# A fused decoder step: twelve gate-projection tiles placed between the attention units, keys without zero padding, sample values turned

## Time and profile before

| what | us |
|---|---|
| executions (median) | 713.58, 714.10, 723.62 (714.10) |
| profiled execution, its span | 716.92, 715.1 |
| TensorE busy | 667.6 (93%) |
| VectorE, ACT, POOL busy | 372.2, 271.4, 150.2 |
| TensorE on the chain that ended last | 51% of the span |
| stages: projection, attention, gates, tail | 255.6, 187.5, 256.0, 16.0 |

### The profile page before, as it was taken

How to read it: one execution, slowest core, us unless ns; L and a number is a source line. 1 busy time by engine, 2 the same in 40 slices (tenths; PEclk the granted TensorE clock), 3 DMA queues, 4 the chain that set the end, 5 groups by cost and what they waited for, 6 DMA issues and landing times.

```text
span 715.1 us, 12634 instructions
## 1 busy us (share of the span) xinstructions
PE 667.6 (93%) x4396; PEld 533.8 (75%) x4396; DVE 372.2 (52%) x999; ACT 271.4 (38%) x629; POOL 150.2 (21%) x219
## 2 busy tenths in 40 slices
PE   4979999998999988999999999999999999999991
PEld 0278676675767866577776768999999999996770
DVE  2054114968976558884786673244232533254537
ACT  5133234242122465664676572333322332221312
POOL 2014450260431544342343331000000000000001
PEclk9969999999999999998999997999999999999997
DMA  9942522422243421002100404223733142322103
GB/s 319 365 140 80 215 85 89 126 85 81 68 121 91 152 90 60 1 2 80 41 1 2 118 2 105 65 68 88 244 88 90 61 118 77 101 60 62 56 1 126
DMA packets 51807, 68.40 MB, mean 96 GB/s; under 512 B 5009, under 2 KB 34889, under 8 KB 51584
## 3 DMA queue, kind: packets, MB, share of 16 engines
q1 hardware_dynamic: 48496, 54.63, 25.4%
q10 hardware_dynamic: 1808, 6.31, 2.6%
q0 software_dynamic: 1440, 6.66, 2.4%
HBM read 62.99 MB, written 6.66 MB: 97 GB/s over the span
## 4 chain that ended last, share of the span: by engine, by line
PE 51%; DVE 3%; issue 1%; ACT 1%; POOL 0%; DVEq 0%; ACTq 0%; POOLq 0%
PE psum L934 26%; PE psum L1117 7%; PE psum L1188 4%; PE psum L1158 3%; PE psum L790 2%; PE psum L1202 2%; PE psum L792 2%; PE psum L791 2%; DVE y L1887 1%; PE psum L1126 1%; PE psum L1138 1%; DVE sig_n L1866 0%; DVE y L1869 0%; DVE sig_d L1839 0%; PE psum L1197 0%
## 5 line engine op out<-in xcount | busy, mean ns | idle before, releaser
L1276 ACT ACTIVATE w_hi<-stage 128x1024 fp32r<-128x1024 f32 (+3 forms) x64 | 63.4, 990 | 202.8 <-PE psum L934 112.7
L1543 DVE TENSOR_TENSOR w_lo<-stage,w_hi 128x1024 fp32r<-128x1024 f32 x40 | 48.9, 1225 | 133.4 <-ACT w_hi L1276 130.0
L790 PE MATMUL psum<-w_hi,hT_hi 128*128 128x512 f32 (+7 forms) x240 | 85.5, 356 | 3.4 <-DVE hT_lo L1518 3.2
L792 PE MATMUL psum<-w_lo,hT_hi 128*128 128x512 f32 (+7 forms) x240 | 84.1, 350 | 0.0
L791 PE MATMUL psum<-w_hi,hT_lo 128*128 128x512 f32 (+7 forms) x240 | 84.0, 350 | 0.0
L766 POOL TENSOR_SCALAR prob<-prob,softmax_stats 128x31 f32<-128x31 f32 (+4 forms) x128 | 62.2, 499 | 97.7 <-DVE softmax_stats L1752 66.4
L934 PE MATMUL psum<-hT_hi,w_hi 128*128 128x272 f32 x384 | 80.5, 291 | 0.3 <-PE psum L1202 0.3
L934 PE MATMUL psum<-hT_lo,w_hi 128*128 128x272 f32 x384 | 80.4, 291 | 0.0
L934 PE MATMUL psum<-hT_hi,w_lo 128*128 128x272 f32 x384 | 80.1, 291 | 0.0
L712 POOL TENSOR_TENSOR w_lo<-stage,w_hi 128x1024 fp32r<-128x1024 f32 (+3 forms) x24 | 45.7, 1905 | 161.8 <-ACT w_hi L1276 161.8
L1411 ACT ACTIVATE prob<-psum,softmax_stats 128x31 f32<-128x31 f32 (+6 forms) x136 | 63.4, 466 | 25.1 <-DVE softmax_stats L1731 13.7
(11 more groups left out here) (295 smaller groups left out, 1207.4 us busy)
## 6 DMA issues: line engine op xcount, KB each, us to landing
stage<-in_w_in SPq DMA_DIRECT2D x14, 1024.0 KB, 5.2
stage<-in_w_ada SPq DMA_DIRECT2D x8, 1024.0 KB, 7.6
stage<-in_w_in SPq DMA_DIRECT2D x10, 512.0 KB, 5.4
stage<-in_w_out SPq DMA_DIRECT2D x4, 1024.0 KB, 5.1
staging<-in_x_prompt ACTq DMA_DIRECT2D x4, 512.0 KB, 5.9
qT_plain<-in_w_ada SPq DMA_DIRECT2D x2, 1024.0 KB, 10.9
qT_rot<-in_w_ada SPq DMA_DIRECT2D x2, 1024.0 KB, 12.5
kz_win_dsa<-in_cache_nsa_kv SPq DMA_DIRECT2D x32, 64.0 KB, 2.4
```

Source lines behind the costliest of these rows:

```text
L790: mm(out, left[0], right[0], start=first, stop=False, skip_group_check=True)
L792: return mm(out, left[0], right[1], start=False, stop=last, skip_group_check=True)
L1276: last = A(dst, src, ACT.Copy)
L1543: last = tt(dst, src, hi.bitcast(F32), ALU.subtract)
```

## The change

Three things are changed together, and the plan of the units with them.

1. **Fills.** z 0, mn 0 and z 1 (twelve tiles of 48 matmuls) leave the gate stage. Each tile is cut into 8 steps of 6 matmuls, and `fill(i)` issues one or two steps (none in K and T units) at the end of iteration i. They accumulate in banks 2 and 3, one tile after the other; ACT copies the raw products to buffers (`fill_raw`) an iteration after a tile's last step, splits the weights' high part one later, and POOL the low part one later again. The scores have banks 0 and 1 only. silu and sigmoid are applied from the buffers in the gate stage, whose jobs are now md 0, un 0, ud 0, mn 1, md 1, un 1, ud 1, y 0, y 1. POOL splits the low parts of all weights.
2. **Unpadded keys.** `kT_*` holds both groups' keys in rows 0-63 and 64-127, and each score matmul contracts over its own 64 rows.
3. **Samples.** The values' operands are exchanged: probabilities are stationary, cached values move (128 columns), and outputs lie on 32 partitions a sequence. A last transpose (`turn_samples`) brings the sum back, after a copy to `oS` by VectorE and before one to `oT`. The sample units are spread over the list instead of following each other, and cached keys and values have one buffer of their own (`cached`), filled by SyncE at fixed places of its list of weights: the first set ahead of the first gate weights, the second ahead of w(mn 0, second half), the next ahead of those of z 1 (first half), z 1 (second half), md 0 (first half) and md 0 (second half).

```diff
+FILL_JOBS = [("z", 0), ("mn", 0), ("z", 1)]
+D_JOBS = [("md", 0), ("un", 0), ("ud", 0), ("mn", 1), ("md", 1), ("un", 1), ("ud", 1), ("y", 0), ("y", 1)]
+JOBS = [("T", i) for i in range(6)] + FILL_JOBS + D_JOBS
...
 def _plan_units():
+    prompt = [("P", b, j, t) for j in range(4) for t in (3, 2, 1, 0) for b in (CMP, SLC, WIN)]
+    prompt += [("P", DSA, j, t) for j in range(4) for t in (3, 2, 1, 0)]
+    before = {2: [("T", DSA), ("K", SLC, 0)], 4: [("S", SLC, 0)], 8: [("K", WIN, 0)], 9: [("S", CMP, 0)],
+              11: [("S", WIN, 0)], 20: [("K", SLC, 1)], 25: [("S", SLC, 1)], 28: [("S", CMP, 1)],
+              31: [("K", WIN, 1)], 34: [("S", WIN, 1)], 44: [("K", DSA, 0)], 49: [("S", DSA, 0)],
+              55: [("K", DSA, 1)], 57: [("S", DSA, 1)]}
...
+def _plan_fill():
+    steps = iter([(f, k) for f in range(N_FILL) for k in range(KT)])
+    out = []
+    for u in UNITS:
+        n = 1 if u[0] == "S" else 0 if u[0] in "KT" else 2 if u[1] != CMP and u[3] >= 2 else 1
+        out.append([x for _, x in zip(range(n), steps)])
+    out[-1] += list(steps)
...
+            def kv_rows(m):
+                b, T = KV_ORDER[m]
+                if m:
+                    sp.wait_ge(pv_done, ORD[KV_READ[m - 1]] + 1)
...
             for i, key in enumerate(LOADS):
+                for m in KV_BEFORE.get(key, ()):
+                    kv_rows(m)
...
+            def bank_free(u, g):
+                if u == 0:
+                    pe.wait_ge(t_dve, NT * (G0 - 1) + g + 1)
+                elif g:
+                    pe.wait_ge(exped, SIG[u])
+                else:
+                    pe.wait_ge(masked if UNITS[u - 1][0] in "KT" else exped, SIG[u - 1] + 1)
...
                 elif kind == "P":
+                    right = (ckT if b == CMP else kT[b])[:, 0:keys(b, t)]
+                    bank_free(u, 1)
+                    for g in range(2):
+                        half = slice(64 * g, 64 * g + 64)
+                        mm(out[g][:, 0:keys(b, t)], left[half], right[half], start=True, stop=True)\
+                            .then_inc(s_done, 1)
...
-                    for s in range(4):
-                        for n in range(2):
-                            last = mm(out[:, 32 * s:32 * s + 32], raw[:, 2 * s + n, P:2 * P],
-                                      pt[:, 0, P * n + 32 * s:P * n + 32 * s + 32], start=False, stop=final,
+                    for n in range(2):
+                        for s in range(4):
+                            last = mm(out[32 * s:32 * s + 32, 0:P], pt[:, 0, P * n + 32 * s:P * n + 32 * s + 32],
+                                      raw[:, 2 * s + n, P:2 * P], start=False, stop=final, skip_group_check=True)
...
+            def fill(i):
+                for f, k in FILL_AT[i]:
+                    n = FIRST[G0] + f
+                    if k == 0:
+                        pe.wait_ge(lo_made, n + 1)
+                        if f:
+                            pe.wait_ge(fill_copied, f)
+                        else:
+                            pe.wait_ge(t_dve, NT * (G0 - 1) + 4)
+                    left = [w_part(x, n, 512).rearrange("p (k n) -> p k n", k=KT) for x in range(2)]
+                    for w, m in ((0, 0), (1, 0), (0, 1)):
+                        for h in range(2):
+                            last = mm(fill_product()[:, h, :], left[w][:, k, :], halves(hT[m][:, k, :])[:, h, :], ...)
+                    if k == KT - 1:
+                        last.then_inc(piece_used, 1)
+
+            def turn_samples(u):
+                for w, n in LAST_OF.items():
+                    if n == u and OWNERS[w][0] in "ND":
+                        T = OWNERS[w][1]
+                        pe.wait_ge(oS_laid, SAMPLE_OWNERS.index(w) + 1)
+                        pe.transpose(owner_bank(w)[:, P:2 * P], oS[:, T, :], ident).then_inc(oS_turned, 1)
...
+            for i in range(len(UNITS) + LAG + 3):
                 if i < len(UNITS):
                     scores(i)
                 if 0 <= i - LAG < len(UNITS):
                     turn(i - LAG)
                 if 0 <= i - LAG - 1 < len(UNITS):
                     values(i - LAG - 1)
+                turn_samples(i - LAG - 2)
+                if i < len(UNITS):
+                    fill(i)
...
+                for f in range(N_FILL):            # ACT, at the start of iteration i
+                    if FILL_END[f] + 1 == i:
+                        act.wait_ge(piece_used, FIRST[G0] + f + 1)
+                        own()
+                        A(halves(fill_raw(f)), fill_product(), ACT.Copy).then_inc(*tell(fill_copied))
...
+                for f in range(N_FILL):            # ACT, at the end of iteration i
+                    if FILL_END[f] + 2 == i:
+                        split_hi(FIRST[G0] + f + 2)
```

More of the change, by code:

```diff
@@ L1097, in scores @@
                 kind, b = unit[:2]
-                out = [bank[(AT[u] + g) % 4] for g in range(2)]
-                bank_free(AT[u])
+                out = bank[0:2]
+                bank_free(u, 0)
                 if kind in "PS" and b == DSA:
@@ L1173, in values @@
                 w = owner(unit)
[L1174 removed]
+                out = owner_bank(w)
                 first = u == FIRST_OF[w]
@@ L1178, in values @@
                 pe.wait_ge(pt_dve, ORDP[u + 1])
-                if first and w >= 2:
-                    pe.wait_ge(o_copied, w - 1)
+                if first:
+                    same = [x for x in range(w) if slot_of_owner(x) == slot_of_owner(w)]
+                    if same:
+                        pe.wait_ge(o_copied, COPIED.index(same[-1]) + 1)
                 pt = probT[:, ORD[u] % 2]
@@ L1191, in values @@
                     for s in range(4):
-                        last = mm(out[:, 32 * s:32 * s + 32], cvS[0:NCS, 4 * unit[2] + s, :],
-                                  pt[0:NCS, 0, 32 * s:32 * s + 32], start=(first and s == 0), stop=final,
-                                  skip_group_check=True)
+                        last = mm(out[32 * s:32 * s + 32, 0:P], pt[0:NCS, 0, 32 * s:32 * s + 32],
+                                  cvS[0:NCS, 4 * unit[2] + s, :], start=first, stop=final, skip_group_check=True)
@@ L1388, in _ @@
                     kind, b = UNITS[i][:2]
-                    src = [bank[(AT[i] + g) % 4] for g in range(2)]
+                    src = bank[0:2]
                     s = stats[:, i % 4, :]
@@ L1696, in mask_max @@
                 kind, b = UNITS[u][:2]
-                src = [bank[(AT[u] + g) % 4] for g in range(2)]
+                src = bank[0:2]
                 s = stats[:, u % 4, :]
```

379 lines of the change are left out of this document (188 added, 191 removed).

## The result

| kernel | executions, median (range) | profiled, span | ratio to the kernel before, 95% |
|---|---|---|---|
| before, same chip | 716.05 (713.58 to 723.62) | 716.92, 715.1 | |
| after | 732.2 (727.2 to 735.52) | 730.43, 728.6 | 1.0201 [1.0143, 1.0259] |

The forecast was 717 us (699 to 740). The time is in the range, in its slower half. The kernel after is slower than the kernel before, but the interval of the ratio, 1.4 to 2.6%, lies on both sides of the 2% that the prediction took as the least difference to be told from no change.

A forecast was written before the change was run, and what follows sets the result against it. The prediction took attention and gate stage to be bound by TensorE's throughput; savings on scores, samples, idle time and clock were offset by seams and new waits, summing to +3 us on the 714.1 median: 717 us (699 to 740).

The forecast's parts named there:

- halves -29: Attention scores: unpadded matmuls on two 64-row halves run side by side with full overlap, saving 29 us.
- seams +22: Attention on TensorE: two more array-shape changes at 0.17 us in each of 64 prompt units, costing 22 us.
- samples -11: Sample units in attention: turned value matmuls of 128 columns replace those of 32 columns, saving 11 us.
- start: Start of attention: first cached keys' loads go ahead of the first gate weights and delay them, costing 2.5 us.
- cached keys: Single cached-key buffer: TensorE stops 5 us for the first samples' window keys, about 1 for the last set; +6 us.
- product pair: Fills' banks 2 and 3: four waits of about 1.5 us where one tile ends and the next begins; +6 us.
- samples: As a wait: four stops of about 1.4 us for turned sums, 2.2 once for the samples' bank; +8 us.
- two score banks: Attention scores wait for both exponentials of the unit before, with two banks instead of four; +13 us, bounds 4 and 25.
- clock: Half-speed spells begun in 32-column sample values vanish, one spell may return; -6 us (0 to -8.5).
- Cheap seams: Rival: 64-row shape entered under other work (-13), two-bank waits fall into fill steps (-7); 697 us, chance 0.20.
- The halves don't overlap: Rival: score row halves don't run at once, 29 us of gain gone, seams kept; 746 us, chance 0.13.
- The softmax chain sets the pace: Rival: scores' wait for the previous unit's exponentials holds attention, costing 20 us more; 737 us, chance 0.17.

The follow-up runs named there:

- k3: The kernel after with the samples' values as before (32 probability columns moving, no turn of the sum): 732.8 us, ratio 1.0240 to the kernel before.
- k11: The kernel before with only the samples' values turned round (probabilities stationary, 128 columns of cached values moving): 703.3 us, ratio 0.9816.
- k1: The kernel before with only the score matmuls changed, each contracting over its own 64 rows; four score banks, no fills: 720.8 us, ratio 1.0108.
- k14: The kernel after with four moves against waits (samples' turn, window keys, fill tiles, first cached keys), its matmul order kept: 707.0 us, ratio 0.9899.
- k13: k9 with a sixth move, the last cached keys and their unit two prompt units later: 699.8 us, ratio 0.9781 to the kernel before.
- k4: The kernel after with 84 of the 96 fill steps left out, copies, splits and waits kept: 734.2 us, ratio 1.0273 to the kernel before.
- k15: k13 with each prompt score matmul over all 128 rows instead of its own 64: 714.9 us, ratio 0.9952 to the kernel before.
- k12: The kernel before with turned sample values and score matmuls on their own 64 rows; four score banks, no fills: 705.7 us, ratio 0.9880.
- k2: The kernel after with each score matmul reading all 128 rows instead of 64: 739.3 us, ratio 1.0315 to the kernel before.
- k5: The kernel after with TensorE's order changed to scores, transposes, fill, samples' turn, values (one seam fewer): 727.8 us, ratio 1.0122 to the kernel before.
- k9: The kernel after with k5's order and four moves against waits (samples' turn, window keys, fill tiles, first cached keys): 702.0 us, ratio 0.9782 to the kernel before.
- k10: The kernel before with only its score banks cut from four to two; padded keys, no fills: 775.2 us, ratio 1.0814.

## Why the prediction was nearly right

**The mechanism held.** Side by side, in the prediction's order (us, profiled executions):

| step | forecast | measured |
|---|---|---|
| work of attention: fills +72, halves -29, seams +22, samples -11 | +54 | +56.0 |
| gate stage, without the clock | -72 | -71.4 |
| - start | +2.5 | first scores at 258.06, 2.5 behind 255.6; idle 5.6, since the projections end 3.3 earlier |
| - cached keys | +6 | 4.8 (window keys) and 0.7 for other keys; the last set in time |
| - product pair | +6 | four stops, 1.8, 1.8, 1.2, 0.8: 5.6 |
| - samples | +8 | four turns 5.0, and 2.0 for the bank |
| - two score banks | +13 | scores 12.7 and first fill 1.5: 14.2 |
| idle in all, after less before | +27 | 38.0 - 8.7 = +29.3 |
| clock | -6 | attention +5.7, gate stage -2.8: +2.9 |
| end of the projection stage | 0 | -3.3 |
| sum (work, gate stage, idle, clock, projection) | +3 | +13.5 |

The gate stage and the tail lost 74.2 us in all; 2.8 of it is a spell of half clock that the stage no longer inherits, listed under clock. The end of the projection stage lay between 250.7 and 255.6 us in the traces of all these kernels, which have the same matmuls there; why is open. That it came 3.3 us early was luck for the sum.

The +56.0 us of work also hides two errors that cancel. The turned samples are worth 8 us of work and not 11 (k3, k11), and the halves with the seam behind them 21.4 and not 29 - 11 = 18 (k1), because that seam costs 0.09 us and not 0.17. The rest of the work was not taken apart.

**The step that was mis-sized is the clock.** The prediction let one new spell "like the 3.4 or 6.8 us ones" come back. Its reading of the earlier trace rows was right (k11: the spells in the 32-column matmuls went), but there were four new spells, 34.1 us. Each begins in or within 2 us behind a stop of a kind that the prediction itself had priced: 256.2 in the start (5.6 us), 273.3 behind the scores' wait of 1.05 that ended at 273.02, 300.6 in the wait for the window keys (4.8 us), 379.1 behind the product pair's 1.83 (which ended at 377.65). It charged each stop for its own length and not for the half clock that follows. In k14, with the stops shortened or gone and the same work, the loss is 6.0 us instead of 12.9; in k13 it is 2.7, with 6.8 us at half clock, in the start. The clock makes 9 of the 10.5 us by which the profiled sum was off (719.9 against 730.4); the other rows add 4.9 and the projection stage takes 3.3 off. The rest of the distance to the median is that the profiled execution of after is 1.8 us below its median, where the forecast put it 2.8 above, and that of before on this chip was 716.05, not 714.1.

**Idle time and half clock.** The kernel before stood at half clock for 14.9 us of attention with 8.7 us idle, the kernel after for 34.1 with 38.0, and k4 for 126.3 with 79.7. The Trainium skill (TensorE: Matmul & The Clock Gate, What's actually happening) says that the gate goes by how busy TensorE has been. The traces agree in direction. They don't make a price list of stops: two stops of 1.83 us in the same kernel were followed by none (288.07) and by 10.2 us (377.65), and k13 has 24.3 us of idle time with one spell. With 22 us idle the loss was 2.5 us in k15, which has fills, and 12.5 in k12, which has none.

**The rivals.** *Cheap seams* fell: the 64-row shape is entered and left at 0.09 us each (k2), half of the price that the forecast took but not nothing, and the two-bank waits came in full. *The halves don't overlap* fell: 512 keys cost 1.06 us. *The softmax chain sets the pace* is half true. The waits of L1180 for L1507 are 9.0 us, near the forecast's, not the 20 more that the rival wanted. But where TensorE is relieved, waits for the chain and half clock together take back over half (k5, k14 to k9) or all (k1, k12), and without the fills the chain shows in full (k4: 47.5 us). A reading that fits all of these, though no run isolates it, is that the fills stand where TensorE would otherwise wait for the chain: so the halves are worth nothing without fills, 7 us with fills and stops, and 12 to 17 us with fills and without stops.

**Where the expected gain is.** By the ratios, the parts on their own come to -13 us (k11), +8 (k1) and +58 (k10). The two score banks are the price of the fills' pair of banks. The parts sum to +53 us and the whole change with its fills came to +14, so the fills pay most of it back. What made the kernel slower than before was four kinds of stop that small moves shorten or remove (k9, k14). But the gain over the kernel before has to be read against k11: the turned sample values alone, with nothing else changed, reach 0.9816 [0.9755, 0.9877], and the whole change with six moves 0.9781 [0.9724, 0.9838]. The two can't be told apart. So the runs don't show that fills and halves, with all their moves, gain anything beyond the turned values.

## What to carry to other kernels

Charge a new stop of TensorE with the half clock behind it as well as with its length, and look for it first where a load or a freed bank is requested just one step too late. Before work is taken off an engine, see in the trace who waits next: taking 21 us off TensorE gave nothing until other work stood in the waits for the softmax chain. Price a change of a ring by running it alone: four score banks to two give 14 us of waits beside the fills, but 30 us of idle time and 57 us in all alone. And run the simplest part of a change by itself before the rest is tuned: here it had the whole gain that can be shown.

## What the runs showed that I had not expected

- Matmuls on the two row halves of the array start 6 ns apart and 512 keys take 1.06 us for both groups instead of 1.82. Each change between this 64-row shape and the full array costs 0.09 us (k2); one between full-height 64-column values and the full array costs 0.17 (k5).
- Removing 76 us of TensorE work (k4) changed the time by less than the measurement can tell (734.2 against 732.2 us): 41.7 us came back as idle time and 35.7 as loss to clock.
- Spells of half clock began at sixteen value matmuls of 32 columns with almost no idle time before them (k1: 13.7 us from 329.1, with 0.3 us idle in the 7 us before); with sixteen of 128 columns in their place none began there (k11).
- A wait that ends before the last result is out shows neither as idle time nor in the list of waits: k10 has 11.4 us of it, in longer distances between starts alone (256 keys: 1.19 us instead of 0.97).
